# Both input projections of a two-block layer in scaled float16 halves, with the weights loaded a chunk ahead into two raw buffers

## The reference, cut to what matters

```python
# block 1
x = layer_norm(x, ln_in_g, ln_in_b)
h = einsum('bsd,de->bse', x, w_in[0])          # the first input projection
au, av, ag, ba, bb, bg, cq, ck, cv, cg = split(h, split_points)
ya = mixer_spatial_gating(au, av, ag, ...)      # 128x128 mixing per head
yb = mixer_conformer_conv(ba, bb, bg, ...)      # 31 taps, depthwise
yc = mixer_window_attention(cq, ck, cv, cg, ...)
y  = einsum('bse,ed->bsd', concatenate([ya, yb, yc]), w_out[0])
x  = layer_norm(DEEPNORM_ALPHA * x + y, post_ln_g[0], post_ln_b[0])
# block 2
h = rmsnorm(x, norm_pre_g)
z = einsum('bsd,de->bse', h, w_in)              # the second input projection
q, k, v, g_attn, c_h, c_b, c_c, g_conv = split(z, cuts)
# rope on q and k, three dilated window attentions, softmax mix of them, silu gate;
# causal 3-tap convolution, silu gate; then w_out_2, rmsnorm and the residual
```

## Time and profile before

| | |
|---|---|
| median of 3 runs | 2439.32 us (2439.11 to 2441.82) |
| the profiled execution's own time | 2441.73 us |
| its span | 2439.9 us |
| mean TensorE clock granted | 0.95 |
| PE busy | 2158.1 us (88%), 16150 matmuls |
| DVE, ACT, POOL busy | 1409.8, 836.8, 774.2 us |
| chain that ended last, by engine | PE 55%, DVE 16%, POOL 11%, issue 7%, DMA 6%, ACT 2% |
| of it, `pe_dense` (L167) | 52% |

### The profile page before, as it was taken

One profiled execution on the slowest core, in us unless ns is written; L12 is line 12 of the kernel. 1 busy time (PEld: TensorE's weight loads), 2 busy tenths in 40 slices (PEclk: granted clock), 3 DMA queues, 4 the chain that ended last, 5 costly groups with the idle time before them and its releaser, 6 DMA issues.

```text
span 2439.9 us, 42721 instructions
## 1 busy us (share of the span) xinstructions
PE 2158.1 (88%) x16150; PEld 1895.7 (78%) x16150; DVE 1409.8 (58%) x3482; ACT 836.8 (34%) x1922; POOL 774.2 (32%) x760
## 2 busy tenths in 40 slices
...
GB/s 152 132 118 52 108 66 46 59 121 176 157 110 100 87 113 98 143 79 79 136 130 114 134 82 57 65 26 70 90 150 180 173 165 152 143 181 151 138 141 110
DMA packets 285628, 279.91 MB, mean 115 GB/s; under 512 B 39936, under 2 KB 237952, under 8 KB 285168
## 3 DMA queue, kind: packets, MB, share of 16 engines
...
## 4 chain that ended last, share of the span: by engine, by line
PE 55%; DVE 16%; POOL 11%; issue 7%; DMA 6%; ACT 2%; SPq 2%; POOLq 0%; DVEq 0%; ACTq 0%
PE bank L167 52%; DVE bank L744 4%; DVE s2m L2035 4%; DVE p2l L2041 3%; DMA woR<-in_w_out 2%; POOL cm L1913 1%; POOL qs L2081 1%; PE bank L371 1%; POOL gt L1921 1%; POOL kept L1917 1%; POOL kept L1915 1%; POOL wol L1252 1%; POOL kept L1913 1%; POOL yo L2264 1%; DMA yn<-scr_y 1%
## 5 line engine op out<-in xcount | busy, mean ns | idle before, releaser
L1978 PE MATMUL bank<-ident,p2r 128*128 128x128 f32 x900 | 170.8, 304 | 90.4 <-DVE p2l L2041 86.7
L167 PE MATMUL bank<-xl,w2h 128*128 128x512 f32 x640 | 249.2, 389 | 0.0
L167 PE MATMUL bank<-xh,w2h 128*128 128x512 f32 x640 | 249.1, 389 | 0.0
L167 PE MATMUL bank<-xh,w2l 128*128 128x512 f32 x640 | 249.1, 389 | 0.0
L167 PE MATMUL bank<-w2h,xh 128*128 128x256 f32 x768 | 219.3, 286 | 10.4 <-issue 9.2
L167 PE MATMUL bank<-w1h,xh 128*128 128x256 f32 x768 | 223.4, 291 | 0.0
L167 PE MATMUL bank<-w1l,xh 128*128 128x256 f32 x768 | 219.8, 286 | 0.0
L167 PE MATMUL bank<-w1h,xl 128*128 128x256 f32 x768 | 219.6, 286 | 0.0
L167 PE MATMUL bank<-w2l,xh 128*128 128x256 f32 x768 | 218.7, 285 | 0.0
L167 PE MATMUL bank<-w2h,xl 128*128 128x256 f32 x768 | 218.7, 285 | 0.0
L1978 PEld LDWEIGHTS bank<-ident,p2r 128*128 128x128 f32 x900 | 102.7, 151 | 140.9 <-DVE p2l L2041 139.2
...
## 6 DMA issues: line engine op xcount, KB each, us to landing
...
qr<-qf SPq DMA_DIRECT2D x192, 64.0 KB, 2.0
v<-scr_v SPq DMA_DIRECT2D x176, 65.0 KB, 2.2
...
```

Of the source, the lines that this page charges most:

```text
L167: ins = nc.tensor.matmul(dst, x, y, start=k == 0 and m == 0, stop=k == n - 1 and m == 2)
L1978: ins = nc.tensor.transpose(bank[:, w * hh + 128 * c:w * hh + 128 * c + 128], p[:, hh, 128 * c:128 * c + 128], ident[:])
```

## The change

- `xh`, `xl`, and the weight halves become float16 (`FH`). So that both halves stay in range, weights and activations are scaled. A chunk's weights are multiplied by 2^14 / sqrt(sum of their squares), the activations by 2^14 / (a bound on |x|), and every reader of a bank multiplies by the inverse (`un`, or `us` with the reader's constant in it).
- The sum of squares is an ACT activation over the raw chunk with an accumulated output (`act_sum`; its 128x2048 result goes into `hi` as scratch). `pool_scale` adds it over the partitions (PARTITION_ALL_REDUCE) and then works out the scales in six small POOL instructions, each waiting for the one before.
- A later chunk's weights are then scaled in place on ACT (`act_scale`) before POOL splits them; the first three are scaled by `act_hi` and `dve_lo` as they are split.
- `dve_most` and the new `dve_widest`, `pool_widest`, `dve_widened` make the bound on |x| and the gain and shift divided by it (`fitted`), before the first transpose.
- In the norm stages the rounding to `xh` moves from ACT to POOL (a CAST for each of 64 pieces); `xf` has four buffers. `act_hi(0)` and `dve_lo(0)` stand behind the third piece of turn 0, `dve_bound(0)` behind the eighth.
- `raw` has two buffers with a semaphore each; `sp_load` runs a chunk further ahead.
- The first constants (ident, gain, shift) are issued from ACT's queue, no longer SP's.

```diff
-            self.raw = sb(f"{tag}r", [128, 8, 256], scope=scope)
-            self.hi = sbs(f"{tag}h", 2, [128, 8, 256], FR, scope)
-            self.lo = sbs(f"{tag}l", 2, [128, 8, 256], FR, scope)
+            self.raw = sbs(f"{tag}r", 2, [128, 8, 256], F32, scope)
+            self.hi = sbs(f"{tag}h", 2, [128, 8, 256], FH, scope)
+            self.lo = sbs(f"{tag}l", 2, [128, 8, 256], FH, scope)
...
         def sp_load(self, n):
-            if n > 0:
-                sp.wait_ge(*self.ready[n - 1])
+            if n > 1:
+                sp.wait_ge(*self.ready[n - 2])
...
-        def act_hi(self, n):
+        def act_sum(self, n):
             act.wait_ge(*self.landed[n])
             if n > 1:
                 act.wait_ge(*self.spent[n - 2])
-            nc.scalar.activation(self.hi[n % 2][:], self.raw[:], ACT.Copy).then_inc(*self.a_w.up())
+            nc.scalar.activation(self.hi[n % 2][:], self.raw[n % 2][:], ACT.Square, accum_out=self.size[:, n, 0:1]).then_inc(*self.a_n.up())
+
+        def pool_scale(self, n):
+            one, total, root, by = self.size[:, n, 0:1], self.size[:, n, 1:2], self.size[:, n, 2:3], self.size[:, n, 3:4]
+            pool.wait_ge(*self.summed[n])
+            nc.gpsimd.partition_all_reduce(total, one, 128, bass.bass_isa.ReduceOp.add).then_inc(*self.g_u.up())
+            pool.wait_ge(*self.g_u.now())
+            nc.gpsimd.tensor_scalar(total, total, 1e-30, None, ALU.max).then_inc(*self.g_u.up())
+            pool.wait_ge(*self.g_u.now())
+            pool.wait_ge(*POWER)
+            nc.gpsimd.tensor_tensor(by, total, power[:, 0:1], ALU.pow).then_inc(*self.g_u.up())
+            pool.wait_ge(*self.g_u.now())
+            nc.gpsimd.tensor_tensor(root, total, by, ALU.mult).then_inc(*self.g_u.up())
+            pool.wait_ge(*self.g_u.now())
+            nc.gpsimd.tensor_scalar(by, by, HTOP, None, ALU.mult).then_inc(*self.g_u.up())
+            pool.wait_ge(*self.widened)
+            nc.gpsimd.tensor_scalar(self.un[n], root, self.wide, 1.0 / HTOP, ALU.mult, ALU.mult).then_inc(*self.g_u.up())
+            pool.wait_ge(*self.g_u.now())
+            nc.gpsimd.tensor_scalar(self.us[n], self.un[n], self.chunks[n]["scale"], None, ALU.mult).then_inc(*self.g_u.up())
+
+        def act_hi(self, n):
+            act.wait_ge(*self.scaled[n])
+            nc.scalar.activation(self.hi[n % 2][:], self.raw[n % 2][:], ACT.Identity, scale=self.size[:, n, 3:4]).then_inc(*self.a_w.up())
...
+        def act_scale(self, n):
+            act.wait_ge(*self.scaled[n])
+            nc.scalar.activation(self.raw[n % 2][:], self.raw[n % 2][:], ACT.Identity, scale=self.size[:, n, 3:4]).then_inc(*self.a_w.up())
...
# norm_stage, act_program, "turn"
                         act.wait_ge(*p_tr.at(m + 1))
-                        act.wait_ge(*d_xl.at(m - 1))
-                        act.wait_ge(*gain_ready)
-                        bias = {} if shift is None else {"bias": shift[:, k:k + 1]}
-                        nc.scalar.activation(xf[m % 2][:], bank[:], ACT.Identity, scale=gain[:, k:k + 1], **bias).then_inc(*a_turn.up())
-                        act.wait_ge(*a_turn.now())
-                        nc.scalar.activation(xh[:, k, 512 * g:512 * g + 512], xf[m % 2][:], ACT.Copy).then_inc(*a_xh.up())
+                        act.wait_ge(*d_xl.at(m - 3))
+                        act.wait_ge(*d_gs.at(3 if shift is None else 4))
+                        bias = {} if shift is None else {"bias": fitted[:, 1, k:k + 1]}
+                        nc.scalar.activation(xf[m % 4][:], bank[:], ACT.Identity, scale=fitted[:, 0, k:k + 1], **bias).then_inc(*a_turn.up())
+                        if m == 2:
+                            wts.act_hi(0)
...
# norm_stage, pool_program
+            pool_widest()
             pool_power(0)
             take_over(pool)
             for item in work:
                 if item[0] == "scale":
                     pool_power(item[1])
-                elif item[0] == "load" and not wts.chunks[item[1]]["fast"]:
+                elif item[0] == "turn":
+                    g = item[1]
+                    for k in range(8):
+                        m = 8 * g + k
+                        pool.wait_ge(*a_turn.at(m + 1))
+                        nc.gpsimd.tensor_copy(xh[:, k, 512 * g:512 * g + 512], xf[m % 4][:]).then_inc(*g_xh.up())
+                    if g == 0 and 0 in valued:
+                        pool_bound(0)
+                elif item[0] == "scaled":
                     wts.pool_split(item[1])
-                elif item[0] == "load" and item[1] in valued:
-                    pool_bound(item[1])
+                elif item[0] == "load":
+                    wts.pool_scale(item[1])
+                    if item[1] > 0 and item[1] in valued:
+                        pool_bound(item[1])
```

239 lines of the change are left out of this document (163 added, 76 removed).

## The result

The changed kernel took 2493.4 us (median of 4 runs, 2486.5 to 2500.6) against 2439.2 of the kernel before (4 runs, 2436.1 to 2441.8): a ratio of 1.022, with a 95% interval of 1.019 to 1.026. The forecast was 2460. Its profiled execution took 2490.25 us with a span of 2488.1 and a mean granted clock of 0.929 (0.95 before).

The account below looks back on a forecast made before the run. It took matmul count times pitch as the bound where TensorE is busy, plus the small-work chain before the norm stages' first two turns: 45.3 ("a") + 41.4 ("b") + 1 - 67 = +20.7, so 2460 us, range 2434 to 2486.

Parts of the forecast that it names:

- the pitch: TensorE matmuls: float16 takes 0.216 us at 512 columns and 0.109 at 256, saving 67 us in all.
- what is PE-bound: Stages where shorter matmuls save time: 32.6 us in 512 form; 256 form conv 8.4, "b" 11.6, gate 12.7; spatial 2.
- S: POOL's code load between an all-reduce and the next arithmetic, taken as 7.25 us.
- Rivals 4 and 5: Float16 streams at the old pitch, 2527, chance 0.04; or 512 columns stream far faster, 2220, chance 0.01.
- The spatial stage, -2: Spatial stage: saves 2 us of 8.4 (0 to 4), since its chain runs over POOL and DVE.
- P: POOL's code load before each all-reduce, between 0 and 8.1 us, taken as 7.25.
- Constants at 8.5: Start of stage "a": constants at 8.5 us, the first link of the chain to turn 0 at 21.3.
- It costs nothing there: Conv, rope and gate stages: pool_scale, 17.5 us, with the split 24 to 31, hides beside a chunk's 41 of matmuls.
- A load a chunk ahead gives back 1.2 us: All 27 chunks: TensorE waited once for weights, 1.2 us, so loading ahead can return no more.
- Rival 1: P is nearly free, since nothing in the trace shows it exposed: 2435 us, chance 0.13.
- rival 2: Norm stages: some 12 exposed loads take 4 us each, not 7.25, so faster at 2421; chance 0.10.
- rival 3: Norm stages: POOL's casts collide with DVE, a piece takes 2 us not 1.1, turns 2 and 3 late: 2484; chance 0.12.

Follow-up runs that it names:

- x1: Kernel before with only xh, xl and the weight halves made float16, unscaled, freed room kept empty: 2388.6 us, ratio 0.978.
- x2: Changed kernel with the all-reduces of the scales replaced by a tensor_scalar, each partition going by its own sum or maximum: 2427.7 us, ratio 0.994.
- x9: Changed kernel with a norm stage's first weight loads held until its first power is done: 2493.4 us (one execution).
- x3: Changed kernel with the rounding to xh on ACT again instead of POOL: 2484.3 us, ratio 1.018 to the kernel before.
- x6: Changed kernel with weight loads no longer a chunk ahead, still two raw buffers: 2551.0 us, ratio 1.045 to the kernel before.
- x8: x1 with two raw buffers and every load a chunk ahead, no scaling: 2383.0 us, ratio 0.975 to the kernel before.
- x7: Changed kernel with rounding on ACT and the norm stages' all-reduces replaced by TensorE products with ones, some work reordered: 2402.7 us, ratio 0.984.

## Why the prediction was wrong

The direction and the main mechanism held: code loads on POOL, on the path of both norm stages, outweigh the pitch. The size did not: 20.7 us forecast, 54 measured between the medians (48.2 between the profiled spans), and 2493 lies outside 2434 to 2486. Of the 27.7 us that the forecast is short of the profiled spans, 8.9 are in the conv stage, 6.4 in the spatial stage, 6.9 in the stretch to the end of the gate stage, and 4.1 and 3.8 up to the two turns 1; the others nearly cancel. The steps that failed are the list of what is PE-bound, for these two stages, and the single size of S. By the prediction's own steps:

- **The pitch**: right. 0.216 forecast, 10.36/48 = 0.216 measured; 0.109 both. Rivals 4 and 5 fell with it.
- **"What is PE-bound", the conv stage's 8.4 and 2.2 us: the step with the largest miss.** Up to the stage's end the prediction has 8.5 of them behind the first bias product, and x1 gained 1.5. It took TensorE for the bound in all but the last two "n" chunks. In the first part TensorE only just hides behind DVE's taps: the bias rows come when the taps allow, so that chunk's 4.2 us went into a longer wait, and the lower clock behind the wait took 2.4. Only from there to the last `ain` does the shorter pitch count. Busy for nearly all of a stage is not the same as being its bound.
- **The spatial stage, -2**: +2.9 in x1, +4.4 in the changed kernel. The term left out is POOL's queue at the start of the stage: the split and, in the changed kernel, a load of 8.6 us stand in it. Without the load the stage is 5.6 us shorter (x2). One execution of each was profiled.
- **S as one number, 7.25**: the term of the norm stages that was mis-sized. Beside the weights' transfers it is 7.7 to 11.5 there (x9 shows that the stretching moves with them). Stage "b" pays 4.0 and 4.3 more for it, stage "a" 3.0 and 0.5.
- **P, 7.25**: 5.8 to 6.6. The error had the other sign, 0.7 to 1.4 us a load, five exposed loads ahead of the two turns 1: 6 us back. The row that I took as nearest was of the other direction. The Trainium skill's figure of about 6 us ("GPSIMD Engine Reference", section "2.1 Instruction dispatch") was nearer to what the trace shows.
- **Constants at 8.5**: 11.7. I moved the landing ahead with the issue. Of the 3.2 us 1.9 go with the weights, which are now issued beside them (9.8 with the weights held back, x9); the rest stays open. With S it made turn 0 of "a" 3.5 us late.
- **Pieces at 1.1**: right for most, 1.01, but the cast beside `dve_lo(0)` took 2.67. The load towards the value bound's all-reduce stands behind the last cast, as the prediction had it; that is what x3 saves (9 us between the medians).
- **The lower clock behind a gap, +2.7**: right, the transposes of turn 1 took 6.17 us for the 6.29 forecast. The +2.5 behind chunk 2 was not measured by itself.
- **Chunk 2, +6.9 and +5.7**: waits of 6.3 (`w1l`) and 8.2 (`w2l`). Right in "a", 2.5 short in "b" (a load of 8.9, beside 127 GB/s).
- **"It costs nothing there", the rope and gate stages**: one wait of 3.6 us, at the seam, where the scaling of a stage's first chunk starts only when the stage before has handed over its stores (ACT's sum at 1514.8, split done at 1535.2). The prediction reckoned with the chain's length inside a chunk and not with where it may start.
- **"A load a chunk ahead gives back 1.2 us"**: wrong in both directions. Without it the scaled kernel loses 58 us more (x6), and in the unscaled kernel it gave 5.6 us between the medians, through the start of the spatial stage and not through a wait for weights (x8). A wait of TensorE shows only what reaches TensorE.

Rival 1 (P free) fell, rival 2 (short loads) too. What rival 2 says of the sign holds as far as this: without the loads on the path the change is a gain (x2, x7). At which length of a load it breaks even no run shows. Of rival 3 the mechanism is there and the price is not (x3).
